# Gated linear attention: the summed decays are copied one head ahead into a second buffer, and VectorE makes the decayed queries of both directions in one operation

## The chip, the cores and the metric

The kernel runs on one core of a Trainium2 chip (trn2). The metric is the device time of one execution in microseconds (us). Names of engines as in the profile: PE is TensorE (matmuls), DVE is VectorE, ACT is ScalarE, POOL is GpSimd. All data here are float32 with 128 partitions; "512 wide" is 512 elements in each partition. SBUF is the on-chip memory, PSUM the eight banks of 512 columns into which PE writes.

## The reference, cut to what matters

A block of four layers (window attention, gated delta rule, gated linear attention, window attention), each followed by a convolutional GLU. The change lies in the third layer, in the scan over chunks, which is run in both directions over 512 tokens (256 of context, 256 of the sequence), for 4 heads with 128 key and 256 value channels:

```python
bcum = jnp.cumsum(la, axis=-2)                     # summed log decays
def step(s, inp):
    qi, ki, vi, bi = inp
    rel = jnp.exp(jnp.where(tri, bi[:, :, :, None, :] - bi[:, :, None, :, :], -jnp.inf))
    a = jnp.einsum('bhid,bhjd,bhijd->bhij', qi, ki, rel)
    bl = bi[:, :, -1:, :]
    o = (qi * jnp.exp(bi)) @ s + a @ vi            # qi * exp(bi): the decayed queries
    s = jnp.exp(bl)[:, :, 0, :, None] * s + jnp.einsum('bhjd,bhje->bhde', ki * jnp.exp(bl - bi), vi)
    return s, o
...
o_f, st_f = scan_fn(*fwd_args, s_fwd)
o_b, st_b = scan_fn(*[jnp.flip(t, 2) for t in bwd_args], s_bwd)
```

## The kernel before, in words

Each engine has its own program; they meet by semaphores, and each works strictly in the order of its own program. Tiles of 128 tokens serve as chunks. The matrix `a` cannot be had from one product, since the decay between two tokens depends on the channel. So the kernel splits it into 7 levels (blocks of 64, 32, ... 1 tokens): at each level queries and keys are multiplied by exponentials of their decay relative to a reference in the middle of the block, one product is made, and the part of it that belongs to the level is kept by a mask.

The scan is written as 4 heads of 10 steps (`C_STEPS`), numbered N = 10 * head + step. For each head there are 9 factors M (`C_FACTORS`), one for steps 0, 1, 3, 4, ... 9. By step:

- **Summed decays**: PE's `cumulate` (L1443, 16 matmuls) writes the sums of both directions to PSUM banks 2 and 3. ACT copies them to the SBUF buffer `cb` (L1014), takes the end values `cel` (L1017), and makes factor 0, F0 = exp(sums / tau), straight from the banks (L1019). All three stand in ACT's step 0.
- **Step 0**: PE makes the plain product of queries and keys. POOL multiplies the queries by the two halves of F0 into `cqe` (L718, L719: the decayed queries, which the outputs use a head later).
- **Step 1**: DVE makes the exponents X1 = end - sums in two operations of 512 (L2514, sums from the bank, ends from `cb`), ACT F1 (L1026), POOL two products (L725, L726), which PE transposes in steps 1 and 2 for the states.
- **Steps 3 to 9**: DVE makes exponents X in one operation of 1024 (L2519: the sums from the bank minus references from `cb`), ACT the factors F from them (L1030, L1032), POOL the factored queries `cqf` and keys `ckf` (L725, L726), PE their product (L1495), and DVE, three steps later in its program, keeps the level's part in `cAT` (L2499; L2495 for step 0).

There are two buffers for X and three for F. Between these, the state updates of the head run (PE L1454, then DVE L2479 or L2482, then the next of PE) in steps 5 to 10, so the last three lie between step 8 and step 0 of the next head; the outputs of the head before (PE L1467, L1469, copied by ACT at L1006) stand in steps 2 to 5. DVE's program in step N is: mask of step N-3, exponents of step N, state update of step N-3. In the body of POOL, the next work after the scan is the split of the output projection's weights (L653, L656), which also fills the kernel outside the scan.

Buffers of earlier and later stages share memory: `cX` lies where the high halves of the split weights lie outside the scan.

Of the kernel before, what the change touches and what calls it, by code (L numbers as in the profile page):

```python
# [19 lines left out]
ALU = mybir.AluOpType  # L20
# [6 lines left out]
P = 128  # L27
# [155 lines left out]
def build(nc, a, out):  # L183
    with ExitStack() as ctx:
# [110 lines left out]
        factor_of = lambda h, step: C_FACTORS * h + (step if step < 2 else step - 1)  # L295
        masked_before = lambda N: N // C_STEPS * (C_STEPS - 2) + max(0, N % C_STEPS - 3) + (N % C_STEPS > 0)
# [19 lines left out]
        cb = sb("cb", [P, 2 * (TOK + 8)], at=LN0 + 3 * K4)  # L316
# [120 lines left out]
        cum_ready = sem("cumulated_ready")  # L437
        dx_ready = sem("exponents_ready")
# [5 lines left out]
        kl_ready = sem("turned_keys_copied")  # L444
        x_fin = sem("x_final")
# [190 lines left out]
        def _(eng):  # L636
# [141 lines left out]
        def _(eng):  # L778
# [183 lines left out]
            def linear_attention():  # L962
# [30 lines left out]
                def factor_free(M):  # L993

                    if M >= 3:
                        eng.wait_ge(qf_ready, M - 2)
                        eng.wait_ge(kf_ready, M - 2)

                both = banks[:, 2:4, :]
                for N in range(C_STAGES + C_STEPS + 4):  # L1000
# [7 lines left out]
                    if N < C_STAGES and step != 2:  # L1008
                        M = factor_of(h, step)
                        F = cF[M % 3]  # L1010
                        if step == 0:
                            eng.wait_ge(cum_ready, h + 1)
                            copies = cb[:, 0:2 * (TOK + 7)].rearrange("p (d c) -> p d c", d=2)[:, :, 0:TOK]
                            eng.activation(copies, both, ACT.Copy)  # L1014
                            for d in range(2):
                                end = bank[2 + d].rearrange("p (t n) -> p t n", t=TT)[:, :, (P - 1) * (1 - d)]
                                eng.activation(cel[:, d, h, :], end, ACT.Exp, scale=1.0 / C_TAU)  # L1017
# [185 lines left out]
        def _(eng):  # L1203
# [202 lines left out]
            def linear_attention(l):  # L1406
# [67 lines left out]
                for N in range(C_STAGES):  # L1474
# [8 lines left out]
                    if step > 0:  # L1483
                        eng.wait_ge(kf_ready if step == 2 else qf_ready, M + 1)
# [1319 lines left out]
```

## Time and profile before

| | |
|---|---|
| median of 3 runs | 2655.36 us (2650.93 to 2656.78) |
| the profiled execution's own time | 2652.73 us |
| its span in the profile | 2650.6 us, so 2.1 us lie around it |
| busy share of the span | PE 94%, DVE 44%, ACT 28%, POOL 60% |
| mean granted PE clock | 0.981 of full speed |
| the scan (first copy of the sums to POOL's last product) | 1702.81 to 1802.94 us of the span |
| busy in these 100.1 us | PE 71.3, DVE 67.4, ACT 57.2, POOL 89.1 us |

The busy share is an average over stages with different limits: over the whole program PE is the bound, but in the scan it is busy 71 of 100 us, while POOL is busy 89. Starts in the profile are counted from the start of the span. A group's row gives busy time and mean duration, then the idle time of the engine just before and what ended it.

### The profile page before, as it was taken

Reading aid. Unit: us, or ns where it says so; the run is one execution under the profiler, and the core shown is the slowest. Engines: PE = TensorE matmul, PEld = TensorE weight load, DVE = VectorE, ACT = ScalarE, POOL = GpSimd, SP = SyncE. Lnnn points to the kernel's source line nnn. Section 1 sums busy time; section 2 is a strip of 40 time slices with the busy share of each in tenths; the row PEclk is TensorE's granted clock in tenths of the full one; section 3 lists DMA queues with packets and bytes.
Section 4 is the critical chain, followed back from the end, with each engine's and each line's share of the span. In section 5 each row is a group of like instructions: output and inputs, shape, how many; then the busy total and the mean of one; then the engine's idle time right before and its main releaser. Section 6 shows DMA issues by size and latency. Waiting matters only on the chain.

```text
span 2650.6 us, 43681 instructions
## 1 busy us (share of the span) xinstructions
PE 2499.9 (94%) x15985; PEld 2047.4 (77%) x15985; DVE 1163.4 (44%) x2120; ACT 751.9 (28%) x1539; POOL 1583.5 (60%) x1567
## 2 busy tenths in 40 slices
PE   6999999999999799999999999878999999989997
PEld 4767788887688698778888757866788887678997
DVE  2384411223469677541222330265422223575555
ACT  2263311111541444231111124152311101363332
POOL 2545577775558222457777555685577775655663
PEclk9999999999999899999999999999999999999999
DMA  7345332244523100242224542202432344503552
GB/s 250 113 161 183 109 104 95 96 158 159 177 65 96 32 2 2 95 145 95 95 95 159 174 162 80 64 1 104 136 95 95 99 157 173 193 31 96 185 176 99
DMA packets 217162, 305.07 MB, mean 115 GB/s; under 512 B 7331, under 2 KB 155550, under 8 KB 217023
## 3 DMA queue, kind: packets, MB, share of 16 engines
q1 hardware_dynamic: 190095, 249.66, 28.6%
q10 hardware_dynamic: 26928, 53.48, 5.6%
q8 instruction: 97, 1.59, 0.3%
q14 instruction: 42, 0.34, 0.0%
HBM read 302.07 MB, written 1.05 MB: 114 GB/s over the span
## 4 chain that ended last, share of the span: by engine, by line
PE 79%; DVE 12%; ACT 3%; POOL 3%; issue 2%; DMA 1%; SPq 1%; DVEq 0%; ACTq 0%; POOLq 0%; PEldq 0%
PE bank L1225 42%; PE bank L1934 13%; PE bank L1276 3%; PE bank L1240 2%; PE bank L1965 2%; PE bank L1713 2%; PE bank L1260 2%; PE bank L1763 2%; PE bank L1757 1%; POOL cqf L725 1%; PE bank L1355 1%; PE bank L1331 1%; DVE ast L2130 1%; DVE ztmp L2203 1%; DVE ztmp L2187 1%
## 5 line engine op out<-in xcount | busy, mean ns | idle before, releaser
L656 POOL TENSOR_TENSOR w_lo<-w_raw,w_hi 128x512 fp32r<-128x512 f32 x652 | 856.3, 1313 | 93.7 <-POOL w_hi L653 72.0
L653 POOL TENSOR_SCALAR w_hi<-w_raw 128x512 fp32r<-128x512 f32 x652 | 427.8, 656 | 617.3 <-PE bank L1225 381.7
L1225 PE MATMUL bank<-u_lo,w_hi 128*128 128x512 f32 (+1 forms) x2048 | 758.5, 370 | 10.0 <-DVE u_lo L2051 6.8
L1225 PE MATMUL bank<-u_hi,w_hi 128*128 128x512 f32 (+1 forms) x2048 | 751.6, 367 | 0.0
L1225 PE MATMUL bank<-u_hi,w_lo 128*128 128x512 f32 (+1 forms) x2048 | 751.4, 367 | 0.0
L1225 PEld LDWEIGHTS bank<-u_lo,w_hi 128*128 128x128 f32 x2048 | 389.1, 190 | 90.6 <-issue 18.9
L1225 PEld LDWEIGHTS bank<-u_hi,w_hi 128*128 128x128 f32 x2048 | 388.9, 190 | 63.1
L1225 PEld LDWEIGHTS bank<-u_hi,w_lo 128*128 128x128 f32 x2048 | 389.2, 190 | 61.0
L1934 PE MATMUL bank<-gs_lo,w_hi 128*128 128x512 f32 (+1 forms) x576 | 209.2, 363 | 1.9 <-POOL w_lo L656 1.8
L1934 PE MATMUL bank<-gs_hi,w_lo 128*128 128x512 f32 (+1 forms) x576 | 208.8, 363 | 0.0
L1934 PE MATMUL bank<-gs_hi,w_hi 128*128 128x512 f32 (+1 forms) x576 | 208.8, 363 | 0.0
L2728 DVE TENSOR_TENSOR gs_lo<-g,gs_hi 128x512 fp32r<-128x512 f32 (+1 forms) x88 | 107.6, 1233 | 230.4 <-ACT gs_hi L1172 230.4
L2703 DVE SCALAR_TENSOR_TENSOR cv<-bank,vec,cv 128x510 f32<-128x510 f32 (+1 forms) x88 | 59.6, 677 | 325.6 <-ACT cv L1146 325.4
L1146 ACT ACTIVATE cv<-bank,vec 128x512 f32<-128x512 f32 (+1 forms) x88 | 58.8, 718 | 500.4 <-PE bank L1225 462.1
L2720 DVE TENSOR_TENSOR g<-cv,bank 128x512 f32 (+3 forms) x88 | 50.8, 616 | 197.1 <-PE bank L1225 195.8
L1172 ACT ACTIVATE gs_hi<-g 128x512 fp32r (+3 forms) x88 | 49.4, 574 | 306.1 <-PE bank L1934 249.0
L736 POOL TENSOR_SCALAR ap<-ap,ast 128x512 f32<-128x512 f32 (+1 forms) x48 | 76.3, 1590 | 80.6 <-DVE ast L2141 80.6
L1934 PEld LDWEIGHTS bank<-gs_lo,w_hi 128*128 128x128 f32 x576 | 108.7, 189 | 20.2 <-issue 3.5
L1934 PEld LDWEIGHTS bank<-gs_hi,w_hi 128*128 128x128 f32 x576 | 108.7, 189 | 17.0
L1934 PEld LDWEIGHTS bank<-gs_hi,w_lo 128*128 128x128 f32 x576 | 108.7, 189 | 16.8
L2056 DVE SCALAR_TENSOR_TENSOR x<-bank,gat,x 128x256 f32<-128x256 f32 x112 | 48.6, 479 | 140.9 <-PE bank L1225 74.7
L2089 DVE TENSOR_TENSOR w_lo<-w_raw,w_hi 128x512 fp32r<-128x512 f32 x76 | 68.5, 911 | 89.4 <-ACT w_hi L811 76.0
(350 smaller groups left out, 3755.4 us busy)
## 6 DMA issues: line engine op xcount, KB each, us to landing
w_raw<-in_ffn_w_up SPq DMA_DIRECT2D x88, 1024.0 KB, 5.1
w_raw<-in_ffn_w_down SPq DMA_DIRECT2D x44, 1024.0 KB, 4.9
ada_area<-in_ada_w ACTq DMA_DIRECT2D x39, 1024.0 KB, 15.4
ada_w<-in_ada_w SPq DMA_DIRECT2D x28, 1024.0 KB, 5.2
w_raw<-in_gdn_w_in SPq DMA_DIRECT2D x16, 1024.0 KB, 5.8
w_raw<-in_attn_w_qkv SPq DMA_DIRECT2D x12, 1024.0 KB, 7.9
ada_w<-in_ada_w ACTq DMA_DIRECT2D x12, 1024.0 KB, 6.7
w_raw<-in_gla_w_in SPq DMA_DIRECT2D x12, 1024.0 KB, 5.4
```

The lines of the kernel that those rows point to most:

```text
L653: eng.tensor_scalar(w_hi[:, q, :], src, 1.0, 0.0, ALU.mult, ALU.add).then_inc(pool.own, pool.step())
L656: eng.tensor_tensor(w_lo[:, q, :], src, w_hi[:, q, :].bitcast(F32), ALU.subtract).then_inc(w_split, 1)
L736: eng.tensor_scalar(pj, pj, ast[:, 4, j % 4, 0:1], None, ALU.mult).then_inc(p_ready, 1)
L1146: eng.activation(cv[:, m, T], bank[(PAIR_GATE if pair else 0) + m][:, T], ACT.Identity, bias=vec[:, bass.ds(f + CONVB(l), 1)], scale=vec[: ...
L1225: mm = eng.matmul(bank[banks[m]][:, T], w[:, q, c:c + P], v[:, k, T], start=(k == 0 and n == 0), stop=(k == KT - 1 and n == 2))
L1240: eng.matmul(bank[banks[m]][:, T], w[:, slot, c + m * P:c + (m + 1) * P], u_hi[:, k, T], start=(k == 0 and n == 0), stop=False)
L1260: mm = eng.matmul(bank[banks[m]][:, T], w[:, k // 2, c:c + P], v[:, k, T], start=(k == 0 and n == 0), stop=(k == KT - 1 and n == 2))
L1276: mm = eng.matmul(bank[banks[t]][:, 0:256], v[:, k, t * P:(t + 1) * P], w[:, q, c:c + 256], start=(k == 0 and n == 0), stop=(k == KT - 1 a ...
L1934: mm = eng.matmul(bank[b][:, T], w[:, q, j * P:(j + 1) * P], v[:, s, T], start=(start and q < 2 and n == 0), stop=(stop and q >= 2 and n = ...
L2089: eng.tensor_tensor(w_lo[:, q, :], w_raw[:, s, q * PIECE:(q + 1) * PIECE], w_hi[:, q, :].bitcast(F32), ALU.subtract).then_inc(w_fourth, 1)
L2703: eng.scalar_tensor_tensor(v3(cv[:, m, :], 1, 256), v3(bank[gate + m][:], 0, 255), w0, v3(cv[:, m, :], 1, 256), ALU.mult, ALU.add).then_in ...
L2728: eng.tensor_tensor(gs_lo[:, slot, T], gf, gs_hi[:, slot, T].bitcast(F32), ALU.subtract).then_inc(gs_ready, 1)
```

## The change

Four things are changed, all in the scan. (1) There are two buffers `cb0` and `cb1` for the copied sums, used by heads in turn; the second lies at the place of the split weights' low halves, which are not in use in the scan. (2) PE makes the next head's sums before its step 4 (before: ahead of step 8), and ACT copies them and takes the end values in its step 6 (`sums_copied`); F0 stays in step 0 and still reads the banks. (3) DVE's exponents take the sums from `cb` and no longer from the banks, in step 1 and in steps 3 to 9. (4) POOL's two products for `cqe` are gone. DVE makes both in one operation of 2 x 512 behind X1 in step 1, with the queries read twice; a semaphore of its own (`qe_ready`) releases F0's buffer and PE's outputs.

```diff
-        cb = sb("cb", [P, 2 * (TOK + 8)], at=LN0 + 3 * K4)
+        cb = [sb(f"cb{i}", [P, 2 * (TOK + 8)], at=o) for i, o in enumerate((LN0 + 3 * K4, WH0 + 4 * K4))]
+        c_sums = lambda h: cb[h % 2][:, 0:2 * (TOK + 7)].rearrange("p (d c) -> p d c", d=2)[:, :, 0:TOK]
+        c_refs = lambda h: cb[h % 2][:].rearrange("p (d c) -> p d c", d=2)[:, :, 0:TOK]
...
-                    for f in range(C_FACTORS):
+                    for f in range(1, C_FACTORS):
...
-                        if f == 0:
-                            if h >= 2:
-                                eng.wait_ge(od_ready, C_OD + TT * (h - 1))
-                            eng.tensor_tensor(cqe[:, 0, h % 2, :], cq[:, h, :], F[:, 0], ALU.mult).then_inc(qf_ready, 1)
-                            eng.tensor_tensor(cqe[:, 1, h % 2, :], cq[:, h, :], F[:, 1], ALU.mult).then_inc(kf_ready, 1)
-                            continue
...
+                def sums_copied(h):
+
+                    eng.wait_ge(cum_ready, h + 1)
+                    eng.activation(c_sums(h), both, ACT.Copy).then_inc(cb_ready, 1)
+                    for d in range(2):
+                        end = bank[2 + d].rearrange("p (t n) -> p t n", t=TT)[:, :, (P - 1) * (1 - d)]
+                        eng.activation(cel[:, d, h, :], end, ACT.Exp, scale=1.0 / C_TAU)
...
+                        if step == 6 and h + 1 < C_HEADS:
+                            sums_copied(h + 1)
...
-                    if step == C_STEPS - 2 and h + 1 < C_HEADS:
-                        eng.wait_ge(dx_ready, (C_FACTORS - 1) * (h + 1))
+                    if step == 4 and h + 1 < C_HEADS:
+                        eng.wait_ge(f_ready, C_FACTORS * h + 1)
                         cumulate(h + 1)
...
                         if step == 1:
-                            eng.wait_ge(f_ready, C_FACTORS * h + 1)
+                            eng.wait_ge(cb_ready, h + 1)
...
-                                ins = eng.tensor_tensor(tiles(X[:, d]), end.to_broadcast([P, TT, P]), tiles(bank[2 + d]), ALU.subtract)
+                                ins = eng.tensor_tensor(tiles(X[:, d]), end.to_broadcast([P, TT, P]), sums, ALU.subtract)
...
-                            ins = eng.tensor_tensor(pair(X[:]), pair(both), ref.unsqueeze(3).to_broadcast([P, 2, TOK // (2 * b), 2 * b]),
+                            ins = eng.tensor_tensor(pair(X[:]), pair(c_sums(h)), ref.unsqueeze(3).to_broadcast([P, 2, TOK // (2 * b), 2 * b]),
...
+                        if step == 1:
+                            if h >= 2:
+                                eng.wait_ge(od_ready, C_OD + TT * (h - 1))
+                            eng.wait_ge(f_ready, C_FACTORS * h + 1)
+                            eng.tensor_tensor(cqe[:, :, h % 2, :], cq[:, h, :].unsqueeze(1).to_broadcast([P, 2, TOK]),
+                                              cF[factor_of(h, 0) % 3][:], ALU.mult).then_inc(qe_ready, 1)
```

DVE's program at the change from the first head to the second, before (X is written `cX`; `bank` as an input is PSUM; `cAT` rows are the masks, `cS` rows the state updates):

```order
L2499 COPY_PREDICATED cAT_154<-msk_50,bank 128x512 [waits level_product_read,level_product_ready]
L2514 TENSOR_TENSOR cX0_165<-cb_167,bank 128x512 [waits factors_ready]
L2514 TENSOR_TENSOR cX0_165<-cb_167,bank 128x512
L2482 SCALAR_TENSOR_TENSOR cS_161<-cS_161,cel_172,bank 128x256 [waits states_updated,state_product_ready]
L2499 COPY_PREDICATED cAT_154<-msk_50,bank 128x512 [waits level_product_read,level_product_ready]
L2482 SCALAR_TENSOR_TENSOR cS_161<-cS_161,cel_172,bank 128x256 [waits states_updated,state_product_ready]
L2495 SCALAR_TENSOR_TENSOR cAT_154<-bank,con_49 128x512 [waits level_product_ready]
L2519 TENSOR_TENSOR cX1_166<-bank,cb_167 128x1024 [waits factors_ready]
```

The same place in the changed kernel:

```order
L2507 COPY_PREDICATED cAT_154<-msk_50,bank 128x512 [waits level_product_read,level_product_ready]
L2523 TENSOR_TENSOR cX0_165<-cb1_168 128x512 [waits factors_ready,cumulated_copied]
L2523 TENSOR_TENSOR cX0_165<-cb1_168 128x512
L2535 TENSOR_TENSOR cqe_156<-cq_150,cF0_162 128x2x512 [waits factors_ready]
L2491 SCALAR_TENSOR_TENSOR cS_161<-cS_161,cel_173,bank 128x256 [waits states_updated,state_product_ready]
L2507 COPY_PREDICATED cAT_154<-msk_50,bank 128x512 [waits level_product_read,level_product_ready]
L2491 SCALAR_TENSOR_TENSOR cS_161<-cS_161,cel_173,bank 128x256 [waits states_updated,state_product_ready]
L2503 SCALAR_TENSOR_TENSOR cAT_154<-bank,con_49 128x512 [waits level_product_ready]
L2528 TENSOR_TENSOR cX1_166<-cb1_168 128x1024 [waits factors_ready]
```

The `cqe` operation has come in between X1 and the first state update, and no exponent reads a bank any more: both of its inputs lie in SBUF.

PE's program in the first head from step 6 to step 8, before (L1443 is `cumulate`, L1495 a level's product, L1454 a state's):

```order
L1495 MATMUL bank<-cqf_157,ckf_158 128x128 x3
L1454 MATMUL bank<-cvt_152,ckl_155 128x256 [waits states_updated]
L1443 MATMUL bank<-con_49,cla_153 128x128 [waits exponents_ready]
L1443 MATMUL bank<-con_49,cla_153 128x128 x7
L1495 MATMUL bank<-cqf_157,ckf_158 128x128 [waits factored_queries_ready,factored_keys_ready,turned_keys_copied,level_product_read]
```

PE's program in the changed kernel, steps 3 and 4 of the first head:

```order
L1504 MATMUL bank<-cqf_157,ckf_158 128x128 x3
L1451 MATMUL bank<-con_49,cla_153 128x128 [waits factors_ready]
L1451 MATMUL bank<-con_49,cla_153 128x128 x7
L1504 MATMUL bank<-cqf_157,ckf_158 128x128 [waits factored_queries_ready,factored_keys_ready,turned_keys_copied,level_product_read]
L1504 MATMUL bank<-cqf_157,ckf_158 128x128 x3
```

The eight `cumulate` matmuls have moved four steps up, and wait for F0 of the head instead of for its last exponent.

## Rows read from the trace of the kernel before

**Rows 1.** First line of the page
```profile
span 2650.6 us, 43681 instructions
```

**Rows 2.** Windows, first two heads: busy of each engine, (x) instructions
```profile
1702.81:1727.79 24.98, 14.79 (x88) 12.21 (x86) 14.84 (x19) 14.77 (x39) 22.24 (x18) 0.80 0.01 2
1727.79:1752.45 24.66, 18.77 (x140) 16.62 (x140) 17.06 (x24) 14.36 (x40) 22.24 (x18) 1.00 0.00 1
```

**Rows 3.** Groups by line in the scan, 1702 to 1812 us
```profile
L726 POOL TENSOR_TENSOR ckf<-ck,cF 128x512 f32<-128x512 f32 x32 | 40.8, 1275 | 0.0
...
L2519 DVE TENSOR_TENSOR cX<-bank,cb 128x1024 f32<-128x1024 f32 x28 | 33.5, 1209 | 0.3 <-ACT cF L1032 0.3
```

**Rows 4.** POOL's timeline: start, duration, [idle before <- what ended it]
```profile
1711.11 1.26 POOL L726 TENSOR_TENSOR ckf<-ck,cF 128x512 f32<-128x512 f32 x1
...
1717.88 1.27 POOL L725 TENSOR_TENSOR cqf<-cq,cF 128x512 f32<-128x512 f32 x1 [0.58 <-ACT cF L1032]
...
1721.58 1.28 POOL L726 TENSOR_TENSOR ckf<-ck,cF 128x512 f32<-128x512 f32 x1
...
1726.52 1.27 POOL L726 TENSOR_TENSOR ckf<-ck,cF 128x512 f32<-128x512 f32 x1
...
1735.17 1.27 POOL L725 TENSOR_TENSOR cqf<-cq,cF 128x512 f32<-128x512 f32 x1 [1.63 <-ACT cF L1032]
...
1801.67 1.27 POOL L726 TENSOR_TENSOR ckf<-ck,cF 128x512 f32<-128x512 f32 x1
```

**Rows 5.** DVE's timeline, end of head 0 and start of head 1
```profile
1724.18 0.75 DVE L2499 COPY_PREDICATED cAT<-msk,bank 128x512 f32<-128x512 uint8 x1 [0.31 <-PE bank L1495]
...
1728.54 1.28 DVE L2514 TENSOR_TENSOR cX<-cb,bank 128x512 f32<-128x512 f32 x2 [0.48 <-ACT cF L1019]
1729.75 0.47 DVE L2482 SCALAR_TENSOR_TENSOR cS<-cS,cel,bank 128x256 f32<-128x256 f32 x1
...
1731.90 0.69 DVE L2495 SCALAR_TENSOR_TENSOR cAT<-bank,con 128x512 f32<-128x512 f32 x1 [0.41 <-PE bank L1491]
1732.51 1.21 DVE L2519 TENSOR_TENSOR cX<-bank,cb 128x1024 f32<-128x1024 f32 x1
```

**Rows 6.** ACT's timeline, first head and second
```profile
1702.81 1.02 ACT L1014 ACTIVATE cb<-bank 128x1024 f32<-128x1024 f32 x1 [46.75 <-PE bank L1443]
...
1706.24 1.06 ACT L1026 ACTIVATE cF<-cX 128x1024 f32<-128x1024 f32 x1 [1.35 <-DVE cX L2514]
...
1734.39 0.70 ACT L1032 ACTIVATE cF<-cX 128x256 f32<-128x256 f32 x2
```

**Rows 7.** 784 to 789 us: timeline of POOL and DVE, and line 2257 (ns min/median/max)
```profile
784.76 2.33 POOL L656 TENSOR_TENSOR w_lo<-w_raw,w_hi 128x512 fp32r<-128x512 f32 x1
787.05 1.59 POOL L653 TENSOR_SCALAR w_hi<-w_raw 128x512 fp32r<-128x512 f32 x1
...
784.71 3.45 DVE L2257 TENSOR_TENSOR zN<-zN,zkk 128x1024 f32<-128x1024 f32 x2
...
L2257 DVE TENSOR_TENSOR zN<-zN,zkk x2: 1225/1766/2308, 784.7 to 785.9; 128x1024 f32<-128x1024 f32 x2
```

**Rows 8.** Timeline, 673 to 682 us: POOL and DVE
```profile
673.73 1.61 POOL L656 TENSOR_TENSOR w_lo<-w_raw,w_hi 128x512 fp32r<-128x512 f32 x1
675.32 1.96 POOL L679 TENSOR_SCALAR x<-x,vec 128x512 f32<-128x512 f32 x2
...
680.19 1.52 POOL L679 TENSOR_SCALAR x<-x,vec 128x512 f32<-128x512 f32 x2
...
674.70 1.18 DVE L2051 TENSOR_TENSOR u_lo<-u,u_hi 128x512 fp32r<-128x512 f32 x1
```

**Rows 9.** DVE's timeline, two SBUF inputs while POOL stands still
```profile
779.98 2.35 DVE L2248 TENSOR_TENSOR zN<-zN,zb 128x1024 f32<-128x1024 f32 x2
```

**Rows 10.** PE's clock (third from last) and a level's product, first head
```profile
1706.00:1718.00 12.00, 6.71 (x29) 5.51 (x30) 7.24 (x9) 7.14 (x19) 11.42 (x11) 0.57 0.00 1
...
1712.52 2.04 PE L1495 MATMUL bank<-cqf,ckf 128*128 128x128 f32 x8 [1.42 <-POOL ckf L726]
```

More of the change, by code:

```diff
@@ L437, in build @@
         cum_ready = sem("cumulated_ready")
+        cb_ready = sem("cumulated_copied")
         dx_ready = sem("exponents_ready")
@@ L444, in build @@
         kl_ready = sem("turned_keys_copied")
+        qe_ready = sem("queries_decayed_from_start")
         x_fin = sem("x_final")
@@ L993, in factor_free @@
                 def factor_free(M):
-                    if M >= 3:
-                        eng.wait_ge(qf_ready, M - 2)
-                        eng.wait_ge(kf_ready, M - 2)
-                both = banks[:, 2:4, :]
+                    used = M - 3
+                    if used >= 0 and used % C_FACTORS == 0:
+                        eng.wait_ge(qe_ready, used // C_FACTORS + 1)
+                    elif used >= 0:
+                        eng.wait_ge(qf_ready, made(used + 1))
+                        eng.wait_ge(kf_ready, made(used + 1))
+                both = banks[:, 2:4, :]
+                def sums_copied(h):
[4 more added lines that the diff above has]
+                        eng.activation(cel[:, d, h, :], end, ACT.Exp, scale=1.0 / C_TAU)
+                sums_copied(0)
                 for N in range(C_STAGES + C_STEPS + 4):
@@ L1011, in linear_attention @@
                         if step == 0:
[L1012 to L1017, printed above, removed]
                             factor_free(M)
@@ L1463, in output @@
                     eng.wait_ge(lv_used, masked_before((h + 1) * C_STEPS))
+                    eng.wait_ge(qe_ready, h + 1)
                     eng.wait_ge(st_upd, C_UD + len(C_UPD) * h + max(C_UPD.index((d, st - 1)) for d, st in entering) + 1)
@@ L1483, in linear_attention @@
                     if step > 0:
-                        eng.wait_ge(kf_ready if step == 2 else qf_ready, M + 1)
+                        eng.wait_ge(kf_ready if step == 2 else qf_ready, made(M + 1))
                     if step > 2:
-                        eng.wait_ge(kf_ready, M + 1)
+                        eng.wait_ge(kf_ready, made(M + 1))
                     for t in range(TT):
@@ L2483, in state_update @@
                                                  ALU.mult, ALU.add).then_inc(st_upd, 1)
-                both = banks[:, 2:4, :]
                 for N in range(C_STAGES + C_STEPS + 4):
@@ L2512, in linear_attention @@
                             for d in range(2):
-                                end = tiles(cb[:, d * (TOK + 7):d * (TOK + 7) + TOK])[:, :, (P - 1) * (1 - d)].unsqueeze(2)
-                                ins = eng.tensor_tensor(tiles(X[:, d]), end.to_broadcast([P, TT, P]), tiles(bank[2 + d]), ALU.subtract)
+                                sums = tiles(c_sums(h)[:, d])
+                                end = sums[:, :, (P - 1) * (1 - d)].unsqueeze(2)
+                                ins = eng.tensor_tensor(tiles(X[:, d]), end.to_broadcast([P, TT, P]), sums, ALU.subtract)
                         else:
```

3 lines of the change are left out of this document (2 added, 1 removed).

## The prediction

> **What bounds the scan now.** I read the windows first [rows 2]: in the second head POOL is busy 22.24 of 24.66 us, DVE 17.06, PE 18.77, ACT 14.36. The 18 POOL operations of a head take 22.24 / 18 = 1.235 us each. The groups [rows 3] show POOL's key products with no idle time ahead of them, and DVE's 1024-wide exponents at 1209 ns. Then POOL's timeline [rows 4], for where it does wait. Call P9 the end of POOL's last product of a head: 1726.52 + 1.27 = 1727.79 us for head 0, 1801.67 + 1.27 = 1802.94 for head 3, so 25.05 us for each of heads 1 to 3. A head has two parts:
>
> - The **levels**: 14 POOL operations back to back, 14 x 1.235 = 17.3 us.
> - The **turn** to the next head, from P9 to the first product of step 3: 1735.17 - 1727.79 = 7.38 us. Four POOL operations lie in it, but they don't set its length. That is set by a chain over DVE and PE [rows 5]: X1 until 1728.54 + 1.28 = 1729.82; the state update behind it on DVE until 1730.22; then PE's next state product and step 0's product, which stand behind that update; DVE's step-0 mask at 1731.90, X3 at 1732.51, F3 until 1735.09 [rows 6]. From the end of the update to the mask it is 1.68 us, from there to POOL's start 3.27 us.
>
> 17.3 + 7.4 = 24.7 of the 25.05 us are so accounted for.
>
> **What I expect of the operations.** POOL reads two SBUF inputs in every product. Before, no DVE operation of the scan reads two SBUF tensors: one input is always a bank. After, all exponents and `cqe` do. What happens when both engines do so at once is shown elsewhere in this trace [rows 7]. DVE's first L2257 runs from 784.71 for 1.225 us, unhurried, to 785.94; POOL's L656 began at 784.76 and ended at 787.09, 1.15 us after DVE's end, and took 2.33 us. DVE's second L2257 took 2.308 us, until 788.16: 1.07 us after POOL's end. POOL's next operation ended 0.48 us after that. They take turns; nothing overlaps except some 0.1 us of start. With POOL at rest the same kind of DVE operation, two SBUF inputs and 1024 wide, takes 2.35 us for two [rows 9], as fast as with a bank. So a 1024-wide exponent that falls between two POOL products costs POOL's line 1.07 + 1.15 - 1.235 = 1.0 us.
>
> Who goes first when POOL has its next operation ready at once? In [rows 8] POOL's L656 ends at 675.34 and L679 follows at once, while DVE's L2051 has waited since 674.70. DVE ends at 675.88, and POOL's pair of L679 takes 1.96 us instead of 1.52, the 0.44 us that DVE held it. The one that waited goes first, so DVE gets in after one POOL operation.
>
> The Trainium skill states this as a rule that speaks against the change ("SBUF — State Buffer", section "SBUF: two separate sides"): the port pair that VectorE and GpSimd share is locked for a whole instruction, also by a VectorE operation with two SBUF inputs when GpSimd reads SBUF, and the other fully blocks. The rows agree with it, and by it the sum below is the same.
>
> **Part by part, heads 1 to 3.** Level steps: each of X5 to X9 now comes between POOL products: 5 x 1.0 = 5.0 us. DVE asks for one exponent per factor (a mask starts 1.32 us after a POOL product's end, 1724.18 [rows 5] against 1721.58 + 1.28 = 1722.86 [rows 4], and X follows it by 0.65), so a factor takes 2 x 1.235 + 1.0 = 3.47 us; F is done some 1.4 us after X, ahead of POOL's need, so nothing is added beyond that. X4 still runs while POOL waits for F3, and overhangs it by about 0.1.
>
> The turn: X1 needs no fresh copy any more, so DVE asks for it 1.97 us after step 8's last product, half a microsecond before P9, gets it at P9, and ends at +1.15 (before: +2.03). F1 is ready at +2.25. But `cqe` stands behind X1 on DVE. The trace has no such operation; it is bounded by 1.13 us (half of [rows 9]'s pair) and 2.31 (the one that waited in [rows 7]). POOL is out of work there until F1, so I take 1.13: end at +2.3. Behind it wait the state update (0.47, end +2.75 against +2.43 before) and with it PE's state product and step 0. The turn becomes 2.75 + 1.68 + 3.27 = 7.7 us, 0.3 longer than before, although POOL does two operations less in it. POOL's relief of 2 x 1.235 = 2.5 us a head turns into idle time.
>
> Sum per head: +5.0 + 0.1 + 0.3 = +5.4 us, three times: +16.2.
>
> **Head 0.** ACT's copy of the sums ends at 1703.83 [rows 6]; X1 follows until 1705.15, F1 until 1706.25 (before: 1706.24 + 1.06 = 1707.30), and POOL starts step 1 at 1706.3. X3 gets in after its first product (1707.5 to 1708.6), POOL's second until 1709.75, X4 until 1710.8, step 3's first product until 1711.95, X5 until 1713.0, its second until 1714.2. Before, that was 1711.11 + 1.26 = 1712.37 [rows 4]: +1.8 already, the saving eaten. Four more exponents: +4.0, less POOL's idle 0.58 at 1717.88 that they cover: +3.4. Head 0: +5.2.
>
> **Costs taken as nothing.** The copy of the next head's sums and the end values (about 1.2 us) in ACT's step 6 are hidden by ACT's idle time (busy 14.36 of 24.66 us); POOL needs the next factor well after. Without that cover it would be 1.2 us a head, at most 3.6. PE's `cumulate`, 16 matmuls, stands behind the outputs in steps 3 and 4 instead of ahead of step 8's product; per factor PE now has a microsecond more, so it is hidden at full clock. After head 3 nothing changes: POOL's weight split starts later by the sum.
>
> **Sum.** 5.2 + 16.2 = +21.4 us on the profiled execution's 2652.73 (span 2650.6 [rows 1], 2.1 around it): 2674.1. The median lies 2.6 above that execution, so 2676.8; I say 2677, slower by 0.8%.
>
> A second rule would shift a term: "VectorE: DVE Perf Modes", section on the TRN2 errata, in the Trainium skill charges VectorE 58 fixed cycles for an SBUF source and 120 for a PSUM one, which makes an estimate of 0.065 us less for each exponent moved, or 1.3 us less over the 20 that I count between products. The trace has 1.21 us for either kind, and the measurement decides.
>
> **The rivals.**
>
> 1. *Collision with turns, as summed* (0.66). 2677, own range 2670 to 2686.
> 2. *Collision, and worse* (0.14). Either POOL keeps going while it has factors, and DVE gets in only when it has none: then POOL idles for an exponent and a factor, 2.5 us for one or for two exponents, 1.25 to 2.5 instead of 1.0 for each of 20: +25 to +50. [Rows 8] speak against it, on one pair of operations of unlike kind. Or PE's clock: in head 0 it stood at 0.57 of full between 1706 and 1718 and a product took 2.04 us [rows 10]. If the longer gap of PE in each turn brings that on, the work of steps 3 to 5 (three products, three outputs, `cumulate`), about half of PE's 18.8 us a head [rows 2], would take 18 us against 3 x 3.47 = 10.4 of POOL's: up to +8 a head on top. Together 2683 to 2705.
> 3. *Part of the collisions is hidden* (0.06): exponents fall where POOL waits anyway, as X3 and X4 do. With two or three of five hidden, +8 to +14: 2663 to 2669.
> 4. *No collision* (0.07), because `cqe` and exponents slip into POOL's starts, or only certain shapes contend. Then the turn stays bound by its chain (7.4), head 0 gains about 0.5 us where F3 comes earlier: 2654 to 2656, no change.
> 5. *Faster* (0.07): POOL's line is what counts, and 8 products less are worth 8 x 1.235 = 9.8 us: 2645.5. It decides this way only if exponents don't hold POOL and the chain of the turn isn't binding, that is, if the state update behind X1 is not what PE waits for. [Rows 5] speak against it.
>
> **The numbers.** What this kernel's measurement can tell from no change is about 0.2%, 5.3 us. Slower: cases 1, 2, 3, 0.86; same: case 4, 0.07; faster: case 5, 0.07. The range reaches over cases 3 and 1 into the larger part of 2: 2662 to 2695.
>
> **What the changed profile would show.** Exponents (now two SBUF inputs) at a mean of 1.6 to 2.2 us instead of 1.21; POOL's products at a mean of 1.5 to 1.6 instead of 1.275, with some of 2.3; a factor every 3.4 to 3.5 us in the levels; the turn at about 7.7 us with POOL idle over 2 us before step 1's first product; the scan about 121 us instead of 100.1. If products stay at 1.27 and exponents at 1.21, the collision is not there and the prediction is wrong; if POOL shows pairs without a DVE operation between them and long idle times on ACT's factors, case 2 is the one.

## The result and the profile after

| | before | changed |
|---|---|---|
| median, in turns on one chip | 2653.14 us (4 runs, 2648.19 to 2656.78) | 2674.9 us (4 runs, 2673.7 to 2675.18) |
| ratio | 1 | 1.0082, 95% interval 1.0064 to 1.0101 |
| span of the profiled execution | 2650.6 us | 2673.4 us |
| the scan, first copy of the sums to POOL's last product | 100.1 us | 121.7 us |
| the span outside the scan | 2550.5 us | 2551.6 us |

The change made the kernel slower by 0.82%, and the loss lies in the scan. The span grew by 22.8 us, of which the scan has 21.6. The page of the changed kernel begins:

```profile
span 2673.4 us, 43693 instructions
```

These are its windows, one for each head, with the columns of [rows 2]: the window, its length, then busy us and (x) instructions of PE, its weight loads, DVE, ACT and POOL, PE's clock, DMA share, GB/s.

```profile
1703.85:1734.82 30.97, 16.05 (x88) 13.34 (x86) 21.72 (x21) 15.52 (x39) 26.42 (x16) 0.78 0.01 1
1734.82:1765.08 30.26, 20.79 (x140) 18.84 (x140) 20.27 (x24) 14.44 (x39) 24.50 (x16) 0.91 0.00 1
1765.08:1795.58 30.50, 21.55 (x141) 19.31 (x140) 20.61 (x26) 14.44 (x39) 24.52 (x17) 0.89 0.00 1
1795.58:1825.58 30.00, 19.46 (x125) 17.04 (x124) 19.57 (x26) 12.48 (x35) 24.85 (x17) 0.92 0.00 1
```

POOL does two operations fewer in a head than in [rows 2] (16 against 18) and is busy 2.3 us longer (24.50 against 22.24). The groups by line of the scan say which work grew:

```profile
L725 POOL TENSOR_TENSOR ckf<-ck,cF 128x512 f32<-128x512 f32 x32 | 50.5, 1577 | 0.0
L724 POOL TENSOR_TENSOR cqf<-cq,cF 128x512 f32<-128x512 f32 x28 | 46.8, 1672 | 10.7 <-ACT cF L1038 10.7
L2528 DVE TENSOR_TENSOR cX<-cb 128x1024 f32<-128x1024 f32 x28 | 43.7, 1574 | 0.0
...
L724 POOL TENSOR_TENSOR cqf<-ck,cF 128x512 f32<-128x512 f32 x4 | 5.1, 1270 | 22.0 <-ACT cF L1032 22.0
L2535 DVE TENSOR_TENSOR cqe<-cq,cF 128x1024 f32<-128x1024 f32 x4 | 4.9, 1217 | 0.0
```

The key products went from 1275 to 1577 ns and the exponents from 1209 to 1574 ns, against [rows 3]. The decayed queries themselves take 1217 ns, which means that nothing stood in their way. POOL now waits for factor 1 in each head, 22.0 us with the wait for the scan's start in it. Its two removed products went into the idle time of the turns: 2.32 us ahead of step 1 and 2.81 ahead of step 3 in the turn shown below, where before it was 0.80 ahead of the decayed queries and 1.63 ahead of step 3.

The two timelines of the second head show the taking of turns. POOL first: start, duration, operation, and in brackets the idle time before it with what ended it.

```profile
1732.32 1.27 POOL L724 TENSOR_TENSOR cqf<-cq,cF 128x512 f32<-128x512 f32 x1 [0.39 <-ACT cF L1038]
1733.55 1.27 POOL L725 TENSOR_TENSOR ckf<-ck,cF 128x512 f32<-128x512 f32 x1
1737.13 1.27 POOL L724 TENSOR_TENSOR cqf<-ck,cF 128x512 f32<-128x512 f32 x1 [2.32 <-ACT cF L1032]
...
1742.45 2.34 POOL L724 TENSOR_TENSOR cqf<-cq,cF 128x512 f32<-128x512 f32 x1 [2.81 <-ACT cF L1038]
...
1748.43 1.26 POOL L724 TENSOR_TENSOR cqf<-cq,cF 128x512 f32<-128x512 f32 x1
1749.66 2.25 POOL L725 TENSOR_TENSOR ckf<-ck,cF 128x512 f32<-128x512 f32 x1
1752.23 1.28 POOL L724 TENSOR_TENSOR cqf<-cq,cF 128x512 f32<-128x512 f32 x1 [0.32 <-ACT cF L1038]
1753.46 2.26 POOL L725 TENSOR_TENSOR ckf<-ck,cF 128x512 f32<-128x512 f32 x1
1756.04 1.91 POOL L724 TENSOR_TENSOR cqf<-cq,cF 128x512 f32<-128x512 f32 x1 [0.32 <-ACT cF L1038]
...
1759.13 2.27 POOL L724 TENSOR_TENSOR cqf<-cq,cF 128x512 f32<-128x512 f32 x1
```

DVE in the same head:

```profile
1735.89 1.21 DVE L2535 TENSOR_TENSOR cqe<-cq,cF 128x1024 f32<-128x1024 f32 x1
1737.03 0.47 DVE L2491 SCALAR_TENSOR_TENSOR cS<-cS,cel,bank 128x256 f32<-128x256 f32 x1
...
1739.18 0.69 DVE L2503 SCALAR_TENSOR_TENSOR cAT<-bank,con 128x512 f32<-128x512 f32 x1 [0.41 <-PE bank L1500]
1739.79 1.22 DVE L2528 TENSOR_TENSOR cX<-cb 128x1024 f32<-128x1024 f32 x1
...
1748.87 1.92 DVE L2528 TENSOR_TENSOR cX<-cb 128x1024 f32<-128x1024 f32 x1
```

DVE's exponent of 1748.87 waits for POOL's product in front, which ends at 1749.69, and is done at 1750.79. POOL's next product, ready at 1749.66, takes 2.25 us instead of 1.27. Five products of this head are held so: 2.34, 2.25, 2.26, 1.91 and 2.27 us, together 4.7 us more than five at 1.27. The row of 1737.13 is the turn: POOL stands idle for 2.32 us ahead of step 1, and again for 2.81 us ahead of step 3.

### The profile page after: what moved, and what is told of

Read it like the earlier page. It is cut to its first block, busy times and chain, and to the rows that moved or that the text cites. A ratio compares the mean times of both kernels' runs of the same rounds, so it can differ in the third digit from the quotient of the medians.

```text
span 2673.4 us, 43693 instructions
## 1 busy us (share of the span) xinstructions
PE 2511.6 (94%) x15985; PEld 2057.8 (77%) x15985; DVE 1174.7 (44%) x2124; ACT 751.8 (28%) x1539; POOL 1596.9 (60%) x1559
## 3 DMA queue, kind: packets, MB, share of 16 engines
HBM read 302.07 MB, written 1.05 MB: 113 GB/s over the span
## 4 chain that ended last, share of the span: by engine, by line
PE 78%; DVE 13%; ACT 3%; POOL 3%; issue 2%; DMA 1%; SPq 1%; DVEq 0%; POOLq 0%; ACTq 0%; PEldq 0%
PE bank L1233 42%; PE bank L1943 12%; PE bank L1284 3%; PE bank L1248 2%; PE bank L1772 2%; PE bank L1974 2%; PE bank L1722 2%; PE bank L1268 1%; PE bank L1766 1%; POOL cqf L724 1%; PE bank L1363 1%; PE bank L1339 1%; DVE ast L2139 1%; DVE ztmp L2212 1%; DVE ztmp L2196 1%
```

## The experiments

The changed kernel's parts are numbered as in the section on the change: (1) second buffer, (2) copy one head ahead, (3) exponents from the copy, (4) decayed queries on DVE. "Turn" and "P9" are the prediction's: P9 is the end of POOL's last product of a head, the turn runs from there to its first product of step 3. Every scan here, as above, runs from the first copy of the sums to POOL's last product. Where a median differs from a span's difference by a few us, the scan of the profile carries the reading: the other 2550 us of the program vary from run to run by more than some of these effects (2544.2 to 2555.9 us in the eleven profiles). Each scan is that of one profiled execution, so differences of a microsecond or two between scans are readings of one trace each.

| kernel | scan, us | turns, us | median, us | ratio to before, 95% interval |
|---|---|---|---|---|
| before | 100.12 | 7.38, 7.58, 7.59 | | |
| changed (1+2+3+4) | 121.73 | 7.63, 7.85, 7.66 | 2674.9 | 1.0082, 1.0064 to 1.0101 |
| part 3 alone | 129.05 | 11.03, 9.49, 9.23 | 2681.93 | 1.0099, 1.0077 to 1.0121 |
| part 4 alone | 108.08 | 9.88, 8.73, 8.73 | 2660.31 | 1.002, 1.0008 to 1.0032 |
| changed without part 4 | 125.61 | 8.42, 8.88, 8.42 | 2683.79 | 1.012, 1.0097 to 1.0143 |
| before, update first | 95.98 | 6.24, 6.42, 6.44 | 2647.93 | 0.9981, 0.9971 to 0.9992 |
| changed, update first | 121.31 | 7.66, 7.65, 7.35 | 2669.76 | 1.0067, 1.005 to 1.0084 |
| before + 16 of 512, bank | 100.59 | 7.60, 7.59, 7.60 | 2654.78 | 0.9991, 0.9978 to 1.0005 |
| before + 16 of 512, SBUF | 111.66 | 8.33, 8.87, 7.61 | 2665.29 | 1.0035, 1.002 to 1.005 |
| before + 16 of 1024, bank | 108.23 | 9.85, 7.63, 7.61 | 2661.2 | 1.0024, 1.0011 to 1.0037 |
| before + 16 of 1024, SBUF | 122.12 | 8.52, 8.40, 8.34 | 2678.75 | 1.0079, 1.005 to 1.0108 |

### Part 3 alone: the exponents read the copy

```diff
-   ins = eng.tensor_tensor(pair(X[:]), pair(both), ref..., ALU.subtract)
+   sums = cb[:, 0:2 * (TOK + 7)].rearrange("p (d c) -> p d c", d=2)[:, :, 0:TOK]
+   ins = eng.tensor_tensor(pair(X[:]), pair(sums), ref..., ALU.subtract)
```

(and the same for the two operations of X1.)

> The kernel before with one part of the change alone: all exponents take the sums from the SBUF copy; order, waits and buffers stay. Theory (a DVE operation with two SBUF inputs and a POOL product exclude each other, 1.0 us of POOL's line each): X5 to X9 cost 5.0 us a head, X1, X3 and X4 now also meet POOL's cqe and step-1 products and lengthen the turn by 1 to 3 us, so +24 to +34 us, slower than the changed kernel; exponents at a mean above 1.6 us, POOL's key products above 1.5. Rival (what costs is the early sums, their copy in step 6 or the new waits, not the source of the exponents): within 3 us of before, operations at 1.21 and 1.27 us.

Measured: scan +28.9 us, median 26.7 us above the kernel before's 2655.23. This one edit, which removes and adds no instruction, makes the whole loss and more. The rest of the change gives some of it back: with parts 1 and 2 added the scan is 125.6 us (below), with part 4 as well 121.7. No run has parts 1 and 2 alone.

In its turns both of POOL's decayed-query products and both halves of X1 now contend. POOL's timeline, then DVE's, at the turn after the second head (P9 is 1774.28):

```profile
1775.05 1.77 POOL L718 TENSOR_TENSOR cqe<-cq,cF 128x512 f32<-128x512 f32 x1 [0.77 <-ACT cF L1019]
1776.78 1.72 POOL L719 TENSOR_TENSOR cqe<-cq,cF 128x512 f32<-128x512 f32 x1
...
1775.01 2.36 DVE L2514 TENSOR_TENSOR cX<-cb 128x512 f32<-128x512 f32 x2 [0.48 <-ACT cF L1019]
```

X1 takes 2.36 us where it took 1.28 in [rows 5]: the halves (512 wide) wait in turn for POOL's products. The update behind it ends at P9 + 3.48 instead of P9 + 2.43. That is 1.05 of the 1.9 us that this turn is longer; the rest is PE's product of step 0, which took 1.92 us instead of 1.05 at a granted clock of 0.50. The first turn, 3.65 us longer, lies beyond the 1 to 3 us that I expected: POOL waits 2.51 us ahead of the decayed queries (0.80 before), and X3 meets its products and takes 2.08 us.

### Part 4 alone: the decayed queries on DVE

The kernel before, in which POOL's two products for `cqe` are gone and DVE makes them behind X1; the exponents keep the banks, the copy stays in step 0.

```diff
+   if step == 1:
+       if h >= 2:
+           eng.wait_ge(od_ready, C_OD + TT * (h - 1))
+       eng.wait_ge(f_ready, C_FACTORS * h + 1)
+       eng.tensor_tensor(cqe[:, :, h % 2, :], cq[:, h, :].unsqueeze(1).to_broadcast([P, 2, TOK]),
+                         cF[factor_of(h, 0) % 3][:], ALU.mult).then_inc(qe_ready, 1)
```

> The kernel before with the other part alone: DVE makes cqe in one operation behind X1, POOL's two products are gone; exponents read the banks, sums are made and copied where they were. Theory (the turn is set by DVE's chain, which cqe lengthens by 1.1 us; POOL's relief is idle time): turn 8.5 us instead of 7.4, in all +3 to +5 us, POOL idle over 3 us in a turn. Rival (POOL's line counts): 8 products less give -6 to -10 us.

Measured: scan +8.0 us, turns 8.73 us (9.88 the first), median +5.1 us. POOL has eight products fewer and the kernel is slower: the case "faster" falls, and with it the idea that POOL's sum of work sets the scan. POOL's products stay at 1276 ns and its idle time ahead of step 1 grows:

```profile
1759.47 1.27 POOL L724 TENSOR_TENSOR cqf<-ck,cF 128x512 f32<-128x512 f32 x1 [3.42 <-ACT cF L1032]
```

A turn is 1.15 us longer than before. That is the 1.13 us that the operation adds ahead of the state update in DVE's program, and nothing of POOL's 2.5 us comes back. The first turn has another microsecond, for which see the last section.

The scan's +8.0 us is more than the 3 to 5 I had expected. The turns make up 4.8 of it, and the start of head 0 0.6, where POOL waits 0.65 us for step 3's factor. The other 2.4 us lie in the levels of heads 1 to 3, where POOL waits 0.59 to 0.87 us ahead of step 6 or 7. My number had nothing for that. In each of these heads PE's product of step 4 took 1.77 to 2.04 us instead of 1.13 (1.57 in the last), so the masks, and the exponents behind them, came later. Why PE's clock was lower there (0.88, 0.94 and 0.88 in the mean of heads 1 to 3, against 1.00, 1.00 and 0.93) is open.

### The changed kernel without part 4

```diff
+   if f == 0:
+       if h >= 2:
+           eng.wait_ge(od_ready, C_OD + TT * (h - 1))
+       eng.tensor_tensor(cqe[:, 0, h % 2, :], cq[:, h, :], F[:, 0], ALU.mult)
+       eng.tensor_tensor(cqe[:, 1, h % 2, :], cq[:, h, :], F[:, 1], ALU.mult).then_inc(qe_ready, 1)
+       continue
```

(in POOL's program, and the operation behind X1 taken out of DVE's.)

> The changed kernel with cqe back on POOL in two products, all else as changed. Theory: POOL does the two products in the turn while it would wait for F1, and the turn stays near 7.6 us; in head 0 POOL starts step 1 later by up to 1.3 us. So within 2 us of the changed kernel, +20 to +24 against before. Rival (moving cqe to DVE is worth POOL's time): 8 x 1.235 = 10 us slower than the changed kernel, +32.

Measured: scan 125.6 us, 3.9 above the changed kernel, where I had at most 2; turns 8.42 to 8.88. The turns are 2.6 of the 3.9 us. The end of the update is P9 + 2.6, as in the changed kernel, but two things behind it were missing from my number. In the first and third turn X3 comes while POOL is in its products of step 1, which now stand behind those for `cqe`, and waits. DVE's timeline, first turn:

```profile
1741.06 2.07 DVE L2534 TENSOR_TENSOR cX<-cb 128x1024 f32<-128x1024 f32 x1
```

That is 0.85 us more than the 1.22 of the changed kernel. In the second turn X3 meets nothing, but only because it comes late itself: step 0's product on PE took 1.92 us and not 1.05. PE's timeline, and the window of this product:

```profile
1770.62 1.19 PE L1468 MATMUL bank<-cvt,ckl 128*128 128x256 f32 x2 [1.39 <-DVE cS L2497]
1771.61 1.92 PE L1506 MATMUL bank<-cq,ck 128*128 128x128 f32 x8
```

```profile
1771.50:1773.60 2.10, 2.10 (x10) 2.01 (x10) 0.52 (x2) 0.00 (x0) 2.10 (x2) 0.50 0.00 0
```

The clock stood at 0.50 there, which is 1.2 GHz, and that adds 0.87 us to the chain of the turn.

Head 0 is 0.7 us longer, and the second head's levels 0.75, though five products are held in the changed kernel there and three and a part of a fourth here. POOL waits ahead of that head's step 7 instead:

```profile
1759.39 1.44 POOL L730 TENSOR_TENSOR cqf<-cq,cF 128x512 f32<-128x512 f32 x1 [2.53 <-ACT cF L1044]
```

PE's trace shows what came late: step 3's product took 2.05 us and `cumulate`, which part 2 puts ahead of step 4's product, 2.81, so step 4's product started 3.87 us after POOL had made its operands, and the mask and X7 stood behind it. In the kernel before, it starts 0.15 us after.

Once the exponents contend, moving the decayed queries to DVE gains 3.9 us, whereas by itself it costs 8.0. The parts of this change don't add.

### The state update ahead of X1, in the kernel before

```diff
+   early = N < C_STAGES and step == 1 and N - 3 in STATES
+   if early:
+       state_update(*STATES[N - 3])
...
-   if N - 3 in STATES:
+   if N - 3 in STATES and not early:
```

> The kernel before with one line moved: in step 1 DVE makes the state update of the head before ahead of X1 instead of behind it. Theory (the chain state update, PE's state product, step 0's product, mask, X3, F3 sets the turn): X3 a microsecond earlier, turn 6.3 us instead of 7.4, three turns, -3 us. Rival (POOL's own four operations and its wait for F0 set the turn): no change, turn 7.4 us.

Measured: turns 6.24 to 6.44 us, scan -4.1 us, time lower by 0.19% (interval 0.08 to 0.29%). This tests the chain of the turn from its other side: a 0.47 us update that no longer stands behind X1 (1.28 us) makes the mean turn 1.15 us shorter, where I had expected about that. The first turn runs from 1726.95 to the product of step 3:

```profile
1733.19 1.28 POOL L725 TENSOR_TENSOR cqf<-cq,cF 128x512 f32<-128x512 f32 x1 [0.47 <-ACT cF L1032]
```

POOL's idle time ahead of it is 0.47 us and no longer 1.63. It is the only kernel of the study that is faster than the kernel before by more than its interval, and it has none of the change's parts.

### The state update ahead of X1, in the changed kernel

The same edit.

> The changed kernel with the state update of step 1 ahead of X1 and the decayed queries in DVE's program; nothing else. In the changed kernel the first update waits behind X1 and the decayed queries, and the turn from POOL's last product of a head to its first of step 3 is 7.63 to 7.85 us. My theory (the turn is the chain over DVE's order, PE's state product and X3): the update ends some 0.5 us or more earlier and the three turns become about 7.0 to 7.3 us, the scan 1.5 to 2 us shorter than 121.7, and the levels' interleaving (products at 1.57 us) stays; the time 1 to 3 us below the changed kernel's. Rival (the turn of the changed kernel is bound by the exponents' and decayed queries' holds, not by the place of the update): no change in the turns. Neither comes near the time of the kernel before.

Measured: turns 7.66, 7.65 and 7.35 us, the sum 0.5 us below the changed kernel's, where I had expected 1.2 or more; the scan 0.4 us shorter. The time (ratio 1.0067, interval 1.005 to 1.0084) can't be told from the changed kernel's. Mostly a miss, and its trace says why. DVE's timeline in the second turn (P9 is 1768.90):

```profile
1768.69 0.47 DVE L2491 SCALAR_TENSOR_TENSOR cS<-cS,cel,bank 128x256 f32<-128x256 f32 x1
...
1772.42 0.67 DVE L2503 SCALAR_TENSOR_TENSOR cAT<-bank,con 128x512 f32<-128x512 f32 x1
1773.02 2.09 DVE L2531 TENSOR_TENSOR cX<-cb 128x1024 f32<-128x1024 f32 x1
```

The update now ends 0.26 us after P9 instead of 2.68 (1737.03 + 0.47 against 1734.82), but the mask of step 0 ends only 0.86 us earlier after P9 (4.19 against 5.05): it now stands without a gap behind DVE's own X1, decayed queries, mask and update, while PE's product of step 0 is done 0.9 us before it starts. X3 then meets POOL's two products of step 1. It waits for the second of them, until 1774.02, and takes 2.09 us instead of 1.22. In the changed kernel X3 came just as POOL had run out of work, and met nothing. What the order gives, the collision takes back. In the second head POOL also waits 2.53 us ahead of step 7, behind a late product of step 4, as in the changed kernel without part 4.

### Sixteen added operations of DVE, four forms

To price the collision by itself I added to the kernel before one DVE operation behind each of X5 to X8, in every head. Its result isn't used. Width and source vary:

```diff
+   if 5 <= step <= 8:
+       eng.tensor_tensor(cz[N % 2][:, 0, :], bank[2], ck[:, 0, :], ALU.subtract)          # 512, bank
+       eng.tensor_tensor(cz[N % 2][:, 0, :], cq[:, 0, :], ck[:, 0, :], ALU.subtract)      # 512, SBUF
+       eng.tensor_tensor(cz[N % 2][:], both, ck[:, 0:2, :], ALU.subtract)                 # 1024, bank
+       eng.tensor_tensor(cz[N % 2][:], cq[:, 0:2, :], ck[:, 0:2, :], ALU.subtract)        # 1024, SBUF
```

(one of the four lines in each kernel.)

> The kernel before with one added DVE operation of 512 columns behind each of X5 to X8 (16 in all), one input from a bank, one from SBUF; its result is not used. It measures what the added DVE time alone costs the scan. My theory (only two SBUF inputs hold POOL): POOL's products stay at 1.27 us, the exponents at 1.21, the added operation takes about 0.63 us and is hidden in DVE's waits for the masks, so the scan of 100.1 us changes by less than 2 us and the time stays within 3 us of the kernel before. Rival (any added DVE work costs, because DVE's chain from mask to exponent is the pace of the levels): +0.6 per operation, about +10 us.

> The same 16 added operations, 512 wide, but both inputs from SBUF. It follows directly on X (1.21 us, one input from a bank), so it comes up against a POOL product that runs. My theory (turns: a DVE operation with two SBUF inputs goes between two products and costs POOL's line its length less the 0.1 us of overlap at start): 16 x 0.46 = +7.4 us in the scan, POOL's mean product about 1.275 + 7.4 / 72 = 1.38 us, the added operation at a median of about 1.1 to 1.7 us. Rival 1 (two inputs in SBUF alone do not matter, the cost in the changed kernel was bank traffic or DVE length): as the bank form, under 2 us. Rival 2 (a collision costs a fixed amount, about 1.0 us, whatever the width): +16 us.

> The same 16 added operations, but 1024 wide, one input from a bank: 1.2 us each of added DVE time. DVE then needs 0.75 + 1.2 + 1.2 us for a factor against the 2.47 us of POOL's two products. My theory: no hold on POOL's products (1.27 us stay), but the next mask and exponent come later, and F has a margin of about 0.4 us; +2 to +8 us in the scan, showing as POOL's idle time on ACT's factors and not as longer products. Rival (longer DVE operations slow POOL by themselves): POOL's products above 1.35 us.

> The same 16 added operations, 1024 wide, both inputs from SBUF: the size of the changed kernel's exponents. My theory (turns, cost by width): up to 16 x 1.0 us on top of nothing, less what d3 shows as waits that now overlap: +14 to +24 us in the scan, with POOL's products at a mean of 1.5 us and the added operation at 1.5 to 2.3 us. Rival 1 (fixed cost per collision): the same as the 512-wide SBUF form. Rival 2 (no port effect): as the 1024-wide bank form.

The groups of the added operation, of POOL's key products and of its query products in the four kernels, in that order of kernels:

```profile
L727 POOL TENSOR_TENSOR ckf<-ck,cF 128x512 f32<-128x512 f32 x32 | 40.8, 1274 | 0.0
L726 POOL TENSOR_TENSOR cqf<-cq,cF 128x512 f32<-128x512 f32 x28 | 35.6, 1272 | 6.2 <-ACT cF L1033 6.1
...
L2524 DVE TENSOR_TENSOR cz<-bank,ck 128x512 f32<-128x512 f32 x16 | 10.9, 679 | 0.0
```

```profile
L727 POOL TENSOR_TENSOR ckf<-ck,cF 128x512 f32<-128x512 f32 x32 | 45.2, 1411 | 0.0
...
L726 POOL TENSOR_TENSOR cqf<-cq,cF 128x512 f32<-128x512 f32 x28 | 35.6, 1270 | 10.7 <-ACT cF L1033 10.7
...
L2524 DVE TENSOR_TENSOR cz<-cq,ck 128x512 f32<-128x512 f32 x16 | 18.0, 1126 | 0.0
```

```profile
L727 POOL TENSOR_TENSOR ckf<-ck,cF 128x512 f32<-128x512 f32 x32 | 40.8, 1274 | 0.0
L726 POOL TENSOR_TENSOR cqf<-cq,cF 128x512 f32<-128x512 f32 x28 | 35.6, 1273 | 11.2 <-ACT cF L1033 11.1
...
L2524 DVE TENSOR_TENSOR cz<-bank,ck 128x1024 f32<-128x1024 f32 x16 | 19.4, 1211 | 0.0
```

```profile
L727 POOL TENSOR_TENSOR ckf<-ck,cF 128x512 f32<-128x512 f32 x32 | 44.5, 1390 | 0.0
...
L726 POOL TENSOR_TENSOR cqf<-cq,cF 128x512 f32<-128x512 f32 x28 | 37.5, 1340 | 19.2 <-ACT cF L1033 19.2
...
L2524 DVE TENSOR_TENSOR cz<-cq,ck 128x1024 f32<-128x1024 f32 x16 | 27.7, 1729 | 0.0
```

What follows:

- **Only the source matters to POOL.** With a bank as one input POOL's products stay at 1274 ns whatever the width. With two SBUF inputs they grow, and so does the operation: 679 to 1126 ns, 1211 to 1729 ns. Rival "no port effect" falls.
- **A held product grows with the width, the scan much less.** A POOL product that the operation holds for its whole length takes 1.72 us at 512 and 2.25 at 1024 instead of 1.27, so 0.45 and 0.98 more. But SBUF against bank, the scan grows by 11.1 us at 512 and by 13.9 us at 1024, so 0.69 and 0.87 us for an operation. The median ratios lie as the scans do (1.0035 against 0.9991; 1.0079 against 1.0024). I had 0.46 for the narrow one. The rival's fixed 1.0 for both doesn't fit either. At 1024 the scan (+22.0 us) lies in what I had expected, but POOL's mean product is 1.35 us and not 1.5: only one product of a head is held for the whole length.
- **The price has two parts, and I had counted one.** At 512 POOL's key products grow by 4.4 us. The other 6.7 us are idle time of POOL ahead of its query products (10.7 us against 6.2) and of those for `cqe`, while it waits for factors. DVE waits for POOL's product too (0.45 us for each operation), so its next mask and exponent come later. At 1024 POOL's products grow by 5.6 us, and its waiting for factors by 8.0.
- **Which part shows depends on PE.** At 512 the four heads are of two kinds. In the last two, step 3's product on PE took 1.46 and 1.13 us: four POOL products of each head are held, POOL never waits in the levels, and these take 19.16 and 19.14 us, 1.8 more than the 17.3 of an undisturbed head. That is the 0.46 us for an operation that I had. In the first two it took 2.05 us, in the second at a granted clock of 0.50 (window 1741.90 to 1744.00), so mask, exponent and factor came about 0.9 us later: one product is held, and POOL waits 2.9 us in the levels of each, 0.6 of it also in the first head of the bank form. All of the added waiting ahead of query products lies in these two. At 1024 this product takes 2.04 or 2.05 us in all four heads with SBUF inputs, in the bank form 2.05, 1.13, 1.13 and 1.74; so 0.69 and 0.87 are prices of the collision together with a slower PE. Whether the collisions brought the lower clock on, no run shows.
- **DVE's length alone** costs nothing at 512 (+0.5 us) and 8.1 us at 1024, just over the upper end of what I had, 2.5 of them in the first turn; at 1024 DVE's line of mask, exponent and added operation (about 3 us) is longer than POOL's two products.

## Why the prediction was right, point by point

The case taken as the likeliest, collision with turns, is what the runs show: forecast 2677 us, measured 2674.9; forecast +21.4 us in the scan, measured +21.6. That it fits to 0.2 us is in part luck: head 0 is 0.8 above its forecast and the other heads together 0.6 below theirs, and in the levels shorter holds and waits that were not foreseen make up for each other. By its steps:

- **That exponents with two SBUF inputs and POOL's products exclude each other** is shown: part 3 alone does it, and the added operations do it with one source and not with the other. The Trainium skill's "SBUF — State Buffer", section "SBUF: two separate sides", has the rule; the four forms agree with both of its halves, the lock and its condition of two SBUF inputs.
- **1.0 us for an exponent between two products; five in a head.** The head shown has five held products, 4.7 us together, and two idle times of 0.32 us ahead of query products that the prediction put at nothing. The 14 level operations of a head took 22.64 us in heads 1 and 2, against 17.31 and 17.29 before, so 5.3 where 5.1 was forecast: 0.4 less in holds, 0.6 more in waits. The exponents' mean, 1574 ns, lies just under the 1.6 to 2.2 us foretold.
- **The turn.** The prediction bounds the decayed queries below by 1.13 us as half of [rows 9]'s pair; half of 2.35 is 1.18. The operation took 1.21 and began 0.08 before X1's end, so 1.13 was right for what it adds. The turn's terms after P9 (1734.82), forecast and measured: end of the decayed queries 2.3 and 2.28; end of the update 2.75 and 2.68; POOL's first product of step 3 7.7 and 7.63. POOL's idle time ahead of step 1 is 2.32 us. The means of the turns before and after, 7.52 and 7.71, put the growth at 0.2 us, where 0.3 was forecast.
- **Heads 1 to 3** together: forecast +16.2, measured +15.6. Head 3 alone is +4.4; before the change it had 0.7 us more in its levels than its neighbours had.
- **Head 0** is the mis-sized term: forecast +5.2, measured +6.0 (30.97 against 24.98). The first steps went as written: step 3's second product (1713.02 + 2.25) ended 11.4 us after the start of the copy, forecast 11.4. The step that failed is "less POOL's idle 0.58 at 1717.88 that they cover". Four more products are held, 4.0 us as forecast, but the idle time did not vanish: POOL waits 0.32 us and, at 1732.32 above, 0.39 us for factors, 0.7 us where it had waited 0.58. The exponents of these two factors had each waited 0.7 us for a POOL product. POOL's timeline in head 0:

```profile
1713.02 2.25 POOL L725 TENSOR_TENSOR ckf<-ck,cF 128x512 f32<-128x512 f32 x1
...
1718.91 2.25 POOL L725 TENSOR_TENSOR ckf<-ck,cF 128x512 f32<-128x512 f32 x1
1721.48 2.32 POOL L724 TENSOR_TENSOR cqf<-cq,cF 128x512 f32<-128x512 f32 x1 [0.32 <-ACT cF L1038]
1723.76 2.25 POOL L725 TENSOR_TENSOR ckf<-ck,cF 128x512 f32<-128x512 f32 x1
...
1729.65 2.28 POOL L725 TENSOR_TENSOR ckf<-ck,cF 128x512 f32<-128x512 f32 x1
```

- **Costs taken as nothing.** The copy one head ahead held no factor. In ACT's timeline it lies in the gap ahead of an exponent that ends at 1722.67:

```profile
1721.30 1.01 ACT L1006 ACTIVATE cb<-bank 128x1024 f32<-128x1024 f32 x1
...
1722.70 0.72 ACT L1036 ACTIVATE cF<-cX 128x256 f32<-128x256 f32 x2 [0.27 <-DVE cX L2528]
```

PE's `cumulate` (8 instructions in the order of the program, 16 records in the trace) was less well hidden. In heads 1 and 2 step 4's product started at 1751.37 and 1781.93, 2.9 and 3.0 us after POOL had made its operands, where it had been 0.15; `cumulate` stood ahead of it, and so did step 3's product, at half clock:

```profile
1746.16 2.04 PE L1504 MATMUL bank<-cqf,ckf 128*128 128x128 f32 x8 [4.82 <-ACT ckl L1048]
```

The same product before:

```profile
1737.82 1.13 PE L1495 MATMUL bank<-cqf,ckf 128*128 128x128 f32 x8 [2.61 <-POOL ckf L726]
```

The mask waited 1.7 us for step 4's product, X7 stood behind the mask, and POOL waited 0.32 and 0.31 us ahead of step 7. Head 3, which has no `cumulate`, has no such wait; but part 3 alone, whose `cumulate` stands where it was, has one in its second head, so how much of it is `cumulate` and how much the slower PE stays open. In the changed kernel it is 0.3 us a head at most; without part 4 it had a share in the 2.53 us above.

- **What lies around the scan** grew by 1.1 us in the span. The median, on the other hand, didn't lie 2.6 us above the profiled execution: 2674.9 is a little under that one's 2675.15. The two together are most of the 2 us between forecast and result.
- **Fallen rivals.** "POOL keeps going while it has factors" would show pairs of products with none held; the head shown has a held one for each of five exponents. "Faster" falls with part 4 alone. Of "PE's clock" something is there: heads 1 to 3 stand at 0.91, 0.89 and 0.92, head 1 at 1.00 before. The turn shown has its usual 0.69 us mask at P9 + 4.36 for a forecast 4.43, so it cost that chain nothing. In the levels it goes with POOL's waits. Taken over all 44 heads of the eleven profiles, step 3's product on PE took 1.96 to 2.05 us in 23, and in every one POOL waited 0.30 to 0.61 us ahead of step 6; it took 1.64 to 1.74 in three, with waits of 0.18 to 0.32; in the 18 with 1.58 us or less there was none. The changed kernel has 2.04, 2.04, 1.96 and 1.57 us, and the wait in all but the last head; before the change only the first had it. This rival's size, up to 8 us a head, did not come: the seven waits of the changed kernel's levels are 2.3 us together, against 1.1 before.

One thing the sum left out, and it was small here: what DVE's own waiting for POOL costs. In the changed kernel it is in the waits of 0.3 to 0.4 us, three in head 0, two each in heads 1 and 2, none in head 3. With the added operations POOL's waiting was more than half of the growth. In the 512-wide SBUF form it costs where the factor is late already, behind a 2.05 us product of PE, and nothing in the heads where that product was faster. This is a reading of the traces; neither PE's clock nor DVE's slack was varied by itself.

## What to carry to other kernels

Before you move a VectorE input from PSUM to SBUF, look whether the other input is in SBUF too and GpSimd is working at the same time. The move adds no instruction and costs nothing alone, yet here it made both engines' operations wait for one another, about 1 us for each 1024-wide one. Price such a collision on both engines: the held operation, and what comes later on the engine that waited, which costs where its result is only just in time. And when an engine is busy 90% of a stage, find its idle gaps before relieving it: here eight operations taken from POOL only lengthened its gaps, while moving one 0.47 us update ahead of 1.28 us of other work shortened each turn by over a microsecond.

## What was not expected of the hardware

- **A short idle stretch of PE can cost a product at half clock, or not.** In the turns PE waits for the update. Step 0's product follows. In the second turn of the changed kernel without part 4, after 1.39 us of idle, it ran at a granted clock of 0.50 and took 1.92 us; in its first turn, also after 1.39 us, it took 1.05. In part 3 alone it was 1.92 us after 2.25 us of idle and 1.05 after 2.73. In part 4 alone it was 1.91 us after 2.38 us of idle in the first turn, and 1.05 us after 2.56 us in the second. So the gap ahead does not decide it alone; what does is left open. For the turn it is 0.87 us, as much as the whole effect that some edits are made for.
- **A held operation hides under another name.** In the kernels with SBUF operations added, a good part of the price stands in the profile as POOL's idle time "<-ACT cF". The lengthened `cz` of the other engine (1126 against 679 ns) points to the collision, and PE's product of step 3 (2.05 against 1.13 us in the second head) to what made the factor late at the outset.
